# A two-layer hybrid trunk on one core: scaling inside the bank, shifted reads and a reordered head in the first projection

## The reference

```python
def rms_norm(x, g, eps=RMS_EPS):
    xf = x.astype(jnp.float32)
    y = xf * lax.rsqrt(jnp.mean(xf * xf, axis=-1, keepdims=True) + eps)
    return (y * g.astype(jnp.float32)).astype(x.dtype)

def token_shift(x):
    return jnp.pad(x, ((0, 0), (1, 0), (0, 0)))[:, :-1]
...
    p = p + (token_shift(p) - p) * mu
    r, k, v, wd, ad, gd = split_cols(p, RWKV_SIZES)
...
    qkv, b_in, a_in, z = split_cols(p, GDN_SIZES)
    qkv = jax.nn.silu(causal_depthwise_conv(qkv, conv_w))
```

## Time and profile before

| | |
|---|---|
| median of 3 runs | 1593.75 us (1593.73 to 1594.44) |
| the profiled execution | 1590.02 us |
| its span, first to last instruction | 1588.2 us |
| mean granted TensorE clock | 0.97 of full speed |
| TensorE busy | 1480.8 us (93%), 11601 matmuls |
| VectorE, ScalarE, GpSimd busy | 724.6, 601.9, 574.5 us |
| the input projection of layer 0 | 0 to about 239 us |
| TensorE's waits in it | 9.9 for the gains, 4.3 before tile 0, 1.8 before the norm's sums, 6.5 and 1.4 around the head sums, 7.1 at the end |

### The profile page before, as it was taken

How to read it: one execution, slowest core, us unless ns; L and a number is a source line. 1 busy time by engine, 2 the same in 40 slices (tenths; PEclk the granted TensorE clock), 3 DMA queues, 4 the chain that set the end, 5 groups by cost and what they waited for, 6 DMA issues and landing times.

```text
span 1588.2 us, 27117 instructions
## 1 busy us (share of the span) xinstructions
PE 1480.8 (93%) x11601; PEld 1193.2 (75%) x11601; DVE 724.6 (46%) x1065; ACT 601.9 (38%) x866; POOL 574.5 (36%) x266
## 2 busy tenths in 40 slices
PE   5999888989987999999999799996989999999998
PEld 4787568888885788888888588773457888888886
DVE  4787775686655341313222602885843413223131
ACT  4424453243334431313232424547854413233231
POOL 4343331010002344343434323233954343443432
PEclk9999899999978999999999899997999999999999
DMA  4332100000011322323223312220002332323231
GB/s 127 89 93 80 53 27 3 4 3 4 4 55 60 100 90 96 105 81 105 87 98 97 89 54 87 73 80 0 1 28 80 106 97 89 106 79 106 79 106 53
DMA packets 128403, 110.18 MB, mean 69 GB/s; under 512 B 10678, under 2 KB 126512, under 8 KB 128304
## 3 DMA queue, kind: packets, MB, share of 16 engines
q1 hardware_dynamic: 126944, 107.06, 21.6%
q10 hardware_dynamic: 1360, 1.65, 0.3%
HBM read 106.60 MB, written 2.10 MB: 68 GB/s over the span
## 4 chain that ended last, share of the span: by engine, by line
PE 76%; DVE 12%; ACT 7%; issue 3%; POOL 1%; ACTq 1%; DVEq 0%; POOLq 0%
PE ps L476 20%; PE ps L481 20%; PE ps L477 20%; PE ps L602 5%; PE ps L664 2%; DVE lower L1864 2%; DVE lower L1860 1%; POOL lower L2066 1%; DVE upper L1467 1%; PE ps L617 1%; PE ps L610 1%; ACT lower L1368 1%; PE ps L579 1%; PE ps L719 1%; PE ps L822 0%
## 5 line engine op out<-in xcount | busy, mean ns | idle before, releaser
L2034 POOL TENSOR_TENSOR w_lo<-lower,w_hi 128x2048 fp32r<-128x2048 f32 x84 | 387.6, 4614 | 642.0 <-ACT w_hi L1024 642.0
L476 PE MATMUL ps<-h_hi,w_hi 128*128 128x512 f32 x792 | 316.0, 399 | 8.9 <-ACT h_hi L1029 5.9
L477 PE MATMUL ps<-h_hi,w_lo 128*128 128x512 f32 x792 | 314.7, 397 | 0.0
L1024 ACT ACTIVATE w_hi<-lower 128x2048 fp32r<-128x2048 f32 x84 | 160.2, 1907 | 242.8 <-PE ps L481 242.8
L481 PE MATMUL ps<-h_lo,w_hi 128*128 128x512 f32 x792 | 201.6, 395 | 0.4
L476 PE MATMUL ps<-a_hi,w_hi 128*128 128x512 f32 x480 | 189.1, 394 | 0.0
L477 PE MATMUL ps<-a_hi,w_lo 128*128 128x512 f32 x480 | 189.1, 394 | 0.0
L476 PEld LDWEIGHTS ps<-h_hi,w_hi 128*128 128x128 f32 x792 | 150.3, 190 | 46.4 <-issue 11.5
L477 PEld LDWEIGHTS ps<-h_hi,w_lo 128*128 128x128 f32 x792 | 150.4, 190 | 36.1 <-issue 0.5
L481 PEld LDWEIGHTS ps<-h_lo,w_hi 128*128 128x128 f32 x792 | 148.7, 188 | 37.4 <-DVE h_lo L1574 1.7
L1809 DVE TENSOR_TENSOR lower<-lower,ps 128x512 f32<-128x512 f32 x64 | 44.0, 688 | 268.7 <-PE ps L481 268.7
(11 more groups left out here) (352 smaller groups left out, 2092.7 us busy)
## 6 DMA issues: line engine op xcount, KB each, us to landing
lower<-in_mlp_w_dram SPq DMA_DIRECT2D x64, 1024.0 KB, 5.2
lower<-in_ev_w_in_dram SPq DMA_DIRECT2D x30, 512.0 KB, 3.8
lower<-in_od_w_in_dram SPq DMA_DIRECT2D x10, 1024.0 KB, 5.2
lower<-in_ev_w_out_dram SPq DMA_DIRECT2D x4, 1024.0 KB, 5.2
lower<-in_od_w_out_dram SPq DMA_DIRECT2D x4, 1024.0 KB, 5.0
out_dram<-lower SPq DMA_DIRECT2D x4, 512.0 KB, 3.2
lower<-in_od_w_in_dram SPq DMA_DIRECT2D x6, 256.0 KB, 3.8
upper<-in_x_dram ACTq DMA_DIRECT2D x1, 1024.0 KB, 8.4
```

Source lines behind the costliest of these rows:

```text
L476: pe.matmul(o, wh, xh, start=(i_ == 0), stop=False)
L477: pe.matmul(o, wl, xh, start=False, stop=False)
L1024: act.activation(WH[:, u % 2, :, 0:w], RAW[:, u % 2, :, 0:w], ACT.Copy).then_inc(hi_ready, 1)
L2034: pool.tensor_tensor(WL[:, u % 2, :, 0:w], RAW[:, u % 2, :, 0:w], as_f32(WH[:, u % 2, :, 0:w]), ALU.subtract)\
```

## The change

1. **Issues.** ScalarE issues the two gains, then the second half of x. SP issues weight tile 0, the first half of x, weight tile 1 and all other parameters.
2. **The split of x.** ScalarE makes the high part from the bank, not from `XT`; VectorE, after it, copies the bank to `XT` and makes the low part from the bank too. The bank is free after both.
3. **Two tiles at the head.** TensorE does the high passes of tiles 0 and 1, then the low passes of both (`first_tiles`). `lora1` moves ahead of the norm's sums and the parameters in `plan`.
4. **Scaling in the bank.** 1/rms is written back into the bank. `shifted` makes (1 - mu) times the row plus mu times the row moved by one, and the convolution starts from its last tap; both read the bank at a shift and write all columns but the first. The bank is freed by the last of them. `STAGE` and its zeros go.
5. **GpSimd** splits the tiles 0 to 2 before it builds masks and constants. VectorE's wait for these moves behind the K tiles.
6. **ScalarE's end.** The inverse norm of `gk` comes at x = 26, SiLUs 10 and 11 at x = 27 behind the rounding of tile 30.
7. **The hand-over.** TensorE waits for the read of Z's banks; the wait for `bank_read` stands behind the scan stage.

```diff
@@ plan
-        plan = (("par0", 1, 0), ("x", 8, 0), ("lora0", 1, 0), ("norm", 1, 1), ("par1", 1, 0), ("lora1", 1, 0),
+        plan = (("par0", 1, 0), ("x", 8, 0), ("lora0", 1, 0), ("lora1", 1, 0), ("norm", 1, 1), ("par1", 1, 0),
@@ SP
-            sp.dma_start(XIN[:, :, 0:512], x_rows[:, :, 0:512]).then_inc(dma_x[0], 16)
...
                 sp.dma_start(PRAW[:, u % 2, :, 0:w], kmaj(ev[:, col:col + w])).then_inc(pr_full[u % 2], 16)
+                if u == 0:
+                    sp.dma_start(XIN[:, :, 0:512], x_rows[:, :, 0:512]).then_inc(dma_x[0], 16)
+                if u == 1:
+                    parameters()
@@ TensorE
+            def first_tiles():
+                o = [bank_of(tile_q[u]) for u in range(2)]
+                for u in range(2):
+                    pe.wait_ge(pw_lo, u + 1)
+                    for k in range(KT):
+                        pe.wait_ge(p_hi, k + 1)
+                        pe.matmul(o[u], PWH[:, u, k, :], PH[:, k, :], start=(k == 0), stop=False)
+                        pe.matmul(o[u], PWL[:, u, k, :], PH[:, k, :], start=False, stop=False)
+                for u in range(2):
+                    for k in range(KT):
+                        pe.wait_ge(p_read[0], p_reads(pq["x"] + k))
+                        mm = pe.matmul(o[u], PWH[:, u, k, :], PL[:, k, :], start=False, stop=(k == KT - 1))
+                    mm.then_inc(p_filled, 1)
@@
-            tile(0)
+            first_tiles()
@@
-            tile(1)
             tile(2)
@@
-            pe.wait_ge(bank_read, Q0)
-            pe.sem_inc(bank_filled, Q0)
+            pe.wait_ge(p_read[0], p_reads(pq["Z"]))
@@ ScalarE
             for k in range(KT):
-                act.wait_ge(p_read[0], p_reads(pq["x"] + k))
-                act.activation(PH[:, k, :], XT[:, k, :], ACT.Copy, scale=pc("norm1", k)).then_inc(p_hi, 1)
+                act.wait_ge(p_filled, pq["x"] + k + 1)
+                act.activation(PH[:, k, :], bank[(pq["x"] + k) % 8], ACT.Copy, scale=pc("norm1", k)).then_inc(p_hi, 1)
@@ VectorE
+            for k in range(KT):
+                o = bank[(pq["x"] + k) % 8]
                 dve.wait_ge(p_hi, k + 1)
...
+                dve.tensor_copy(XT[:, k, :], o)
+                dve.scalar_tensor_tensor(out=PL[:, k, :], in0=o, scalar=pc("norm1", k), in1=as_f32(PH[:, k, :]),
+                                         op0=mul, op1=sub).then_inc(p_read[0], 1)
@@
-                read0(dve.tensor_tensor(STAGE[:, slot, 3:3 + W], o, RS[0], mul), q)
-                return STAGE[:, slot, :]
...
+                t.link(dve.tensor_tensor(o, o, RS[0], mul))
+                return q, o
@@ convolved
-                stage, dst = staged(name, c, i % 4), GQKV[:, i, :]
-                t.link(dve.tensor_scalar(dst, stage[:, 0:W], pc("conv", i), None, mul))
-                for tap in range(1, 4):
-                    ins = dve.scalar_tensor_tensor(out=dst, in0=stage[:, tap:tap + W], scalar=pc("conv", 12 * tap + i),
-                                                   in1=dst, op0=mul, op1=add)
...
+                t.link(dve.tensor_scalar(dst, o, pc("conv", 36 + i), None, mul))
+                for back in range(1, 4):
+                    ins = dve.scalar_tensor_tensor(out=dst[:, back:W], in0=o[:, 0:W - back],
+                                                   scalar=pc("conv", 12 * (3 - back) + i),
+                                                   in1=dst[:, back:W], op0=mul, op1=add)
```

136 lines of the change are left out of this document (70 added, 66 removed).

## The result

| | before | after |
|---|---|---|
| median of the timed runs | 1593.79 us (1593.73 to 1594.44, 4 runs) | 1572.54 us (1571.45 to 1573.66, 4 runs) |
| the profiled execution | 1590.02 us | 1572.37 us |
| its span | 1588.2 us | 1570.7 us |
| last tile of the projection ends, next stage starts | 231.8, 239.08 us | 222.13, 222.13 us |
| first head products of the scan stage | 251.71 us | 232.52 us |

The account below looks back on a forecast made before the run. TensorE bounds the input projection, losing time only at head, head sums and end. 7.1 + 1.1 + 6.6 + 2.2 = 17.0, less 0.5, gives 16.5 us: 1573.5 profiled, 1577.2 median; range 1573 to 1584.

Parts of the forecast that it names:

- head: Start of the input projection: tile 2 comes 8.1 us earlier, a 1.0 us wait before tile 3 given back; 7.1 us.
- head sums: Waits near 173 to 182 us: tiles resume at 174.5 against 182.27 without tap stretches; 1.1 us beyond the head.
- end: After the last tile: next stage starts at 224.3 instead of 239.08, 14.8 us, less 8.2 already gained.
- warm start: Next stage's first products and transposes run at the full clock instead of after 7.1 us idle; 2.2 us.
- writing PSUM: Allowance of 0.5 us taken off the sum of 17.0 for what VectorE's writing into PSUM may cost.
- The step that failed: Whole time: 1573.5 us for the profiled execution becomes 1577.2, as the median shown lies 3.7 above the profile.
- 1.9 and 1.0: Range's downward allowances: a clock that never falls at the head sums (1.9 us), no stall at tile 3 (1.0).
- Rival 2: Head: first half of x lands as late as 13.2 us, or GpSimd's constants stretch; 13.6 gained, 1580; chance 0.15.
- Rival 5: Head: x itself, not the issues, set it, and only the end moves; 9.4 us gained, 1584; chance 0.05.
- Rival 1: Convolutions: stretches remain because VectorE's output still goes to SBUF; gain 13.5 us, 1580; chance 0.08.
- rival 4: Convolutions: PSUM operations far dearer, held banks stop TensorE; slower, 1597 at 2.0 us an operation; chance 0.03.
- Rival 3: End: stays VectorE's and ScalarE's, their work queuing over 5 us late; about 9 us gained, 1585; chance 0.07.

Follow-up runs that it names:

- Experiment 1: The kernel before run again with nothing edited, with a profile of its own; 1592.03 us, median of nine executions (1587.60 to 1594.07).
- experiment 7: The changed kernel with GpSimd's split of tile 3 before its last constants and ScalarE's rounding of tile 3 before the wait for the norm's sums; 1571.38 us.
- experiment 6: The changed kernel with the first half of x issued on SP's queue ahead of weight tile 0 instead of behind it; 1574.56 us.
- experiment 5: The changed kernel with loads issued as before: SP first half of x first, ScalarE the other half, the gains and 21 parameter loads; 1579.30 us.
- experiment 4: The changed kernel with its twelve convolutions made through the SBUF stage again, as before; 1572.59 us.
- experiment 8: The changed kernel with VectorE's three products of kk moved from between convolutions GK0 and GK1 to behind the bonus products; 1561.37 us.
- Experiment 9: The changed kernel with TensorE waiting, before the scan stage, for the read of Z's last bank instead of its first; 1573.23 us in one execution.
- Experiment 2: The kernel before with the end alone: gk's inverse norm at x = 26, TensorE waiting for Z's first bank read, not the hand-over count; 1582.68 us.
- Experiment 3: The kernel before with 24 additional products on TensorE between its last tile and the wait for VectorE's flag; 1590.50 us.

## Why the prediction was off by as much as it was

In the first column the forecast's terms, in the second what the trace of the changed kernel gives at the same place.

| term | forecast | measured | from |
|---|---|---|---|
| head | 7.1 | 8.4 | last passes of tile 3, 46.68 to 38.28 |
| head sums | 1.1 | 1.3 | last passes of GV0, 187.79 to 178.11, less 8.4 |
| end | 6.6 | 7.3 | stage start, 239.08 to 222.13, less 9.7 |
| warm start | 2.2 | 2.2 | first head products, 251.71 to 232.52, less 16.95 |
| writing PSUM | -0.5 | 0 | scalings into the bank 0.68 to 0.70 us |
| sum | 16.5 | 19.2 | |
| behind it | 0 | -1.7 | same program; the clock |
| profiled executions | 16.5 | 17.65 | |
| medians | 16.5 | 21.2 | |

Between the 19.2 and the 17.65 lie the 1.7 us behind the first head products and, the other way, 0.15 us outside the spans.

**The step that failed** is the last one of the sum: "the median shown is 3.7 above it at 1593.75, which gives 1577.2". It takes the distance between one profiled execution and a median as a constant that the changed kernel would have too. Against 1573.5, the number one line before it, the measured 1572.5 is 1.0 off, and that small number owes something to luck: the gain was 2.7 us too small at the first head products, and 1.7 us of scatter behind them went the other way. Experiment 1 shows that the distance is scatter between executions, and the stretches there show the clock in it: 1587.6 to 1596.4 us for one program. The range named bounds for every cost of the change and none for this, although two numbers 3.7 us apart for one kernel lay on the table; what it names downwards, 1.9 and 1.0, leads from 1577.2 to 1574.3 and not to 1573. The 3.7 alone did not carry the time out of the range: with it and a gain of 19.2 the forecast would have been 1574.5. The mis-sized terms did the rest: the head by 1.3 us, the end by 0.7, writing PSUM by 0.5 and the head sums by 0.2. From the first head products on, thirteen profiles of the same code took 1336.1 to 1340.7 us, mean 1337.6; before's profile was at 1336.5 and the changed kernel's at 1338.2, which is the -1.7. A gain of 19.2 is thus the best single number for the change, and the 19.5 between the means of 46 and of 4 executions agrees with it; 17.65 and 21.2 are it with two draws of the scatter.

**Head.** Right: no gap from the transposes to tile 2, VectorE in time, GpSimd's constants, 21.8 to 32.1 us and not stretched, cost one wait before tile 3. It was said to be 1.0 and measured 1.44, but in the programs with the same head it is up to 2.5 us: it grows as x comes earlier, since GpSimd hardly does (experiment 7). Mis-sized: the landing of x. "It lands near 10.3" adds 2 us to the 8.3 of before. The 2 us were fair (experiment 6: 2.5). The 8.3 was not the right base: before, ScalarE's half of x was issued at the same time. In experiment 6 it follows two gains, at 1.83, and SP's half, issued first as before, lands at 6.2. That ScalarE's later issue is the reason fits this and experiment 5, where both are issued at 0.80 and SP's half takes 7.4 us again; no run moves it alone. The transposes start at 8.73 instead of 10.4, which is 1.7 of the 2.0 us by which tile 2 was early. Rival 2 falls with this: x landed at 8.7, not at 13.2. Rival 5 falls by experiment 5, where the issues and their order are 5.5 us at tile 3.

**Head sums.** A convolution takes 3.74 us, not 3.6, as each operation that reads the bank is 0.06 dearer than the 0.69 taken. In experiment 4's comparison 1.5 us are won, and the order of events is the predicted one: last taps free the banks, TensorE's next tile starts at 173.18 (174.5 said). Rival 1 (stretches remain) is refuted by the changed kernel's trace, with 2.31 to 2.32 us for every three taps, rival 4 (dear PSUM operations) by rows of 0.68 to 0.75 us. The forecast named VectorE as "late" and did not ask with what: with 8.9 us of products out of place, as experiment 8 shows.

**End.** The flag at 212.3 was said to come at 213.7. "The end is now TensorE's own: Z's last bank is read 0.69 after 223.6" misread the change, whose wait names the first Z bank. Experiment 9 puts 1.2 us on that, where the forecast had charged 0.7: this is the 0.7 by which the end is better than said. Rival 3 falls. Experiment 2 isolates the end at 9.4 us, with the warm start; the terms were 7.1 of idle time and 2.2 of clock. That rival 5 also said 9.4 is chance, as its sum has the head sums in it.

**Warm start.** Experiment 3 gives 2.16 for 2.2.

## What to carry to other kernels

When a change is worth 1%, forecast it from one profile to the same place in another, and give the scatter between executions of one program a term of its own in the range: a second profile of the unchanged kernel would have shown it. Where an engine is late for a bank, look first at what it does just before, and who waits for that: moving 9 us of work that was not yet needed behind three convolutions was worth 10.1 us, where convolutions that no longer stretch had given 1.5. And read a semaphore's count in the diff to the number: which of four uses it names decided 1.2 us.

## What was not expected of the hardware

- A program without any change had undisturbed executions from 1587.6 to 1596.4 us on one core, with mean granted clocks of 0.972 in the quickest and 0.962 in the slowest.
- Transposes at the head take 0.23 us each for the first 16 (3.66 us) and 0.12 for the next 16 (1.97 us) in experiment 6, with a granted clock of 1.00 all the while; the 32 of them took 5.25 to 6.56 us from one execution to the next. What makes them slow is open: the clock in the rows does not show it, though 0.23 and 0.12 are close to what they take at the lower and at the full clock later on (0.214 and 0.11). The loads beside them are not it: from 12 to 14 us the changed kernel did six to seven a us at a DMA share of at most 0.05, and the kernel before in experiment 1 eleven a us from 13 to 14 at a share of 1.00.
- A product with three operands in SBUF that is itself tiny (128 x 32) took 2.33 us beside a split on GpSimd and 0.18 us without it: as if it waited until the split was through.
- The landing of 1 MB moves by 2.5 us with its place behind 0.5 MB on its queue (7.4 us from its issue against 5.4), and between executions by 1 us (transposes start at 8.19 to 9.24 us in seven programs with the same issues).
